# Three stacked layers on one core: the modulation's weighted sum moved from TensorE to VectorE, and the last experts' outputs added from 32-row strips

## The reference

```python
x = layer_ab(x, ...)      # norm, projection, two attentions (indexed top-k and sliding window), output projection
x = layer_cd(x, ...)      # norm, projection, compressed / selected / window attention, latent attention, output
mod = silu(c) @ w_ada + b_ada                 # c: 1024 numbers, w_ada: 1024 x 6144
sh1, sc1, g1, sh2, sc2, g2 = split(mod, 6)
h = rms_norm(x, norm1_g) * (1 + sc1) + sh1;   z = h @ w_in
x = x + g1 * (concat([diff_attention(z), multiscale_pool(z)]) @ w_out)
h = rms_norm(x, norm2_g) * (1 + sc2) + sh2
x = x + g2 * hierarchical_moe(h, ...)         # 32 experts of 1024 -> 512 -> 1024, two of them for each token
return rms_norm(x, final_g)
```

## Time and profile before

| | us |
|---|---|
| median of 3 runs | 978.06 (977.4 to 981.19) |
| profiled execution, its own time | 980.98 |
| span of the profiled execution | 978.9 |
| TensorE busy | 817.0 (83% of the span) |
| VectorE busy | 308.2 (31%) |
| ScalarE busy | 170.8 (17%) |

### The profile page before, as it was taken

How to read it: one execution, slowest core, us unless ns; L and a number is a source line. 1 busy time by engine, 2 the same in 40 slices (tenths; PEclk the granted TensorE clock), 3 DMA queues, 4 the chain that set the end, 5 groups by cost and what they waited for, 6 DMA issues and landing times.

```text
span 978.9 us, 13367 instructions
## 1 busy us (share of the span) xinstructions
PE 817.0 (83%) x5617; PEld 477.2 (49%) x5617; DVE 308.2 (31%) x786; ACT 170.8 (17%) x477; POOL 39.7 (4%) x36
## 2 busy tenths in 40 slices
PE   5999899999999899998887998686777767587665
PEld 3544554455567544455454755353444535354332
DVE  1476541127755423125443121211211111111112
ACT  3121540213255401004111010000000000000001
POOL 0110000011600000000000000000000000000000
PEclk9999998999999999999997999897998889998789
DMA  9963791243502475445465999999999999999994
GB/s 345 393 241 121 276 344 59 96 166 118 200 35 98 150 253 187 172 171 204 147 234 213 428 384 428 428 429 428 428 428 428 429 428 428 428 428 427 428 426 163
DMA packets 53387, 284.39 MB, mean 291 GB/s; under 512 B 2656, under 2 KB 7136, under 8 KB 40416
## 3 DMA queue, kind: packets, MB, share of 16 engines
q1 hardware_dynamic: 53344, 283.81, 73.2%
HBM read 282.75 MB, written 1.05 MB: 290 GB/s over the span
## 4 chain that ended last, share of the span: by engine, by line
PE 56%; DMA 33%; DVE 4%; ACT 2%; issue 2%; POOL 1%; SPq 1%; DVEq 0%; POOLq 0%
DMA ring<-in_up_w 30%; PE banks L1627 14%; PE banks L1748 14%; PE banks L2049 7%; PE banks L1707 4%; DMA ring<-in_down_w 3%; PE banks L1729 2%; PE banks L1654 2%; PE banks L1691 2%; PE banks L2095 2%; PE banks L1735 1%; POOL rs L512 1%; DMA ring<-in_ab_w 1%; PE banks L1606 1%; PE banks L2032 1%
## 5 line engine op out<-in xcount | busy, mean ns | idle before, releaser
L2049 PE MATMUL banks<-ring,QT 128*32 128x256 f32 x1952 | 148.1, 451 | 85.4 <-DMA ring<-in_up_w 84.6
L1748 PE MATMUL banks<-ring,hT 128*128 128x512 f32 (+4 forms) x384 | 157.3, 564 | 5.0 <-DMA ring<-in_ab_w 2.5
L2049 PEld LDWEIGHTS banks<-ring,QT 128*32 128x32 f32 x1952 | 78.1, 125 | 153.0 <-issue 95.1
L1627 PE MATMUL banks<-ring,hT 128*128 128x512 f32 x320 | 141.1, 600 | 7.5 <-ACT hT L536 5.1
L1748 PEld LDWEIGHTS banks<-ring,hT 128*128 128x128 f32 x384 | 72.2, 192 | 76.8 <-issue 68.8
L1627 PEld LDWEIGHTS banks<-ring,hT 128*128 128x128 f32 x320 | 60.9, 192 | 82.8 <-issue 76.7
L1518 DVE TENSOR_TENSOR QT<-banks,MOD 32x256 f32<-32x256 f32 x128 | 53.8, 420 | 140.3 <-PE banks L2095 139.0
L2095 PE MATMUL banks<-ring,QT 128*32 128x256 f32 x992 | 68.3, 420 | 15.6 <-ACT QT L828 12.4
L1509 DVE TENSOR_TENSOR QT<-QT,banks 64x256 f32<-64x256 f32 x32 | 13.5, 423 | 198.0 <-ACT QT L821 198.0
L512 POOL TENSOR_TENSOR rs<-st,mhalf 128x1 f32<-128x1 f32 (+7 forms) x27 | 32.5, 1204 | 933.7 <-DVE st L1561 467.1
L821 ACT ACTIVATE QT<-banks 64x256 f32<-64x256 f32 x32 | 12.0, 375 | 299.9 <-PE banks L2049 299.9
(11 more groups left out here) (344 smaller groups left out, 693.5 us busy)
## 6 DMA issues: line engine op xcount, KB each, us to landing
ring<-in_up_w SPq DMA_DIRECT2D x31, 2048.0 KB, 23.4
ring<-in_gate_w SPq DMA_DIRECT2D x30, 2048.0 KB, 18.9
ring<-in_down_w SPq DMA_DIRECT2D x30, 2048.0 KB, 21.8
ring<-in_ada_w SPq DMA_DIRECT2D x12, 2048.0 KB, 9.0
ring<-in_ab_w SPq DMA_DIRECT2D x4, 2048.0 KB, 20.2
ring<-in_cd_w SPq DMA_DIRECT2D x4, 2048.0 KB, 9.4
ring<-in_in_w SPq DMA_DIRECT2D x4, 2048.0 KB, 11.2
ring<-in_ab_out_w SPq DMA_DIRECT2D x2, 2048.0 KB, 10.5
```

The source lines that it names most:

```text
L1627: ins = pe.matmul(bank[j % 4][:, 0:n], hT[:, k, t * P:(t + 1) * P], w[:, k, :], start=(k == 0), stop=(k == KD - 1))
L1748: ins = pe.matmul(bank[b][:, 0:n], hT[:, k, t * P:(t + 1) * P], w[:, k, :], start=(k == 0), stop=(k == KD - 1))
L2049: return pe.matmul(bank[1][CAP * j:CAP * j + CAP, 0:256], XG[:, k, CAP * s:CAP * s + CAP], wk[:, :, 2 * (j % 2):2 * (j % 2) + 2], start=(k ...
```

## The change

Modulation: `ada_parts`, ScalarE's copy and `silu_c` go. VectorE makes the weighted sum of a chunk's eight slices by itself (`weigh`, eight linked operations of 128x512) into one of two halves of `extra`; TensorE's `ada_sum` adds the partitions with `share` = 1. Chunk 0 is weighed before part 0, chunks 1 to 6 beside `about` and `cdin`, 7 to 11 beside `cdout` and `win`, and the sums are placed between the groups of these projections. The load order changes with it.

Experts: for experts 30 and 31 the down product, whose four strips of 32 rows hold the four column quarters, is gated by one operation (`GATE_LAST`, `YE_LAST`) and added by eight 32-row, 256-column matmuls in two waves of four row strips (`add_last`), with the turned weights repeated on four strips (`on_strips`, `turn_last`). Experts 28 and 29 are added before expert 31's gate and up products, with 64 rows. At the end each tile's sum of squares is one operation of 1024.

```diff
-        add_ada(0, 7)
+        add_ada(0, 1)
         add_cols("about", ab_out_w, D)
+        add_ada(1, 7)
         for c in range(3):
             add_piece("cdin", cd_w, CD_AT, CD_WIDTHS, c)
...
-        add_ada(7, 10)
         add_cols("cdout", cd_out_w, D)
+        add_ada(7, 8)
         chunks.append(("rows", [(0, D, 1, norm_rows[:, 0:1]), (D, D, 1, norm_rows[:, 2:3])], ("final_row", 1)))
-        add_cols("win", in_w, 2048)
-        add_ada(10, 11)
+        add_ada(8, 10)
+        add_cols("win", in_w, 2048, (0, 2))
+        add_ada(10, 12)
+        add_cols("win", in_w, 2048, (2, 4))
...
-        add_ada(11, 12)
         add_cols("wout", out_w, D)
...
+            def weigh(c, ks=range(KD)):
+                if ks[0] == 0:
+                    arrived(v, f"ada{c}")
+                    if c > 1:
+                        v.wait_ge(*upto("ada_s", c - 1))
+                w = weights(f"ada{c}")[:, :].rearrange("p (k n) -> p k n", k=KD)
+                acc = ada_acc(c)
+                for k in ks:
+                    by = cs[:, 1, k:k + 1]
+                    if k == 0:
+                        ins = v.tensor_scalar(acc, w[:, k, :], by, None, ALU.mult)
+                    else:
+                        ins = v.scalar_tensor_tensor(out=acc, in0=w[:, k, :], scalar=by, in1=acc, op0=ALU.mult, op1=ALU.add)
+                    link(ins, "ada_mm" if k == KD - 1 else "dve")
...
-            attention(0, after=ada_rows)
-            for t in range(NT):
-                turned_rows("abm", t)
-            add_and_norm("about", "cd", "cdx", col="cd_col")
+            weigh(0)
...
+            attention(0, after=lambda u: ada(0) if u == 4 else None)
+            turned_rows("abm", 0)
+            weigh(1)
+            turned_rows("abm", 1)
+            def beside_first(n):
+                if n == 0:
+                    weigh(2)
+                elif n == 1:
+                    ada(1)
+                    weigh(3)
+                elif n == 2:
+                    ada(2)
+                elif n == 3:
+                    weigh(4, range(0, 4))
+                elif n == 4:
+                    ada(3)
+                elif n == 6:
+                    weigh(4, range(4, 8))
+            add_and_norm("about", "cd", "cdx", col="cd_col", beside=beside_first)
+            weigh(5)
+            ada(4)
+            weigh(6)
+            ada(5)
...
+            turned_rows("cdm", 0)
+            weigh(7)
+            turned_rows("cdm", 1)
...
+            def beside_second(n):
+                if n == 0:
+                    weigh(8)
+                elif n == 1:
+                    ada(7)
+                    weigh(9)
+                elif n == 2:
+                    ada(8)
+                elif n == 4:
+                    ada(9)
+            add_and_norm("cdout", "e1", "e1x", rows_=(1, 0), beside=beside_second)
             link(v.tensor_scalar(MOD[:, 0, :], weights("rows")[:, D:2 * D], math.sqrt(D), None, ALU.mult), "final_row")
+            weigh(10)
+            weigh(11)
...
-                if c is not None:
-                    ada_parts(c)
                 fill(u)
...
-            attention(0, ada_during)
+            attention(0, fill=lambda u: ada_sum(0) if u == 3 else None)
-            project("about", D, first_outputs)
+            project("about", D, first_outputs, ada_sums({1: 1, 2: 2, 3: 3}))
...
+            pe.wait_ge(*upto("about_x", 4))
+            ada_sum(4)
             project_cd(1, 0, 0)
+            ada_sum(5)
...
             project_cd(1, 1, 1)
+            ada_sum(6)
...
-            project("cdout", D, second_outputs)
-            project("win", 2048, normed_rows("e1", "e1x"))
+            project("cdout", D, second_outputs, ada_sums({1: 7, 2: 8, 3: 9}))
+            project("win", 2048, normed_rows("e1", "e1x", 9), ada_sums({1: 10, 3: 11}))
...
+                if e >= NE - 2:
+                    v.wait_ge(*upto("g_gl", 4))
+                    if e == NE - 1:
+                        v.wait_ge(*upto("g_wave", 8))
+                    v.tensor_tensor(YE_LAST, bank[2][:, 0:256], GATE_LAST, ALU.mult).then_inc(sem("g_ye"), 1)
+                    return
...
+            def add_last(i):
+                pe.wait_ge(*upto("g_swc", QUADS + 1 + i))
+                pe.wait_ge(*upto("g_ye", NE - 1 + i))
+                for wave in range(2):
+                    if i or wave:
+                        pe.wait_ge(*upto("g_wave", 8 * i + 4 * wave))
+                    for t in range(NT):
+                        for half in range(2):
+                            n = 2 * half + (t + wave) % 2
+                            strip = slice(CAP * n, CAP * n + CAP)
+                            pe.matmul(bank[4 + 2 * t + half][:, 256 * (n % 2):256 * (n % 2) + 256], SWT_LAST[i][strip, t, :],
+                                      YE_LAST[strip, :], start=False, stop=bool(i and wave))\
+                              .then_inc(sem("sums" if i and wave else "g_wave"), 1)
...
+                    if last_quad(q) and s in (1, 2):
+                        turn_last(s - 1)
                     turn_hidden(q, s)
                     if last_quad(q) and s == 2:
+                        add_outputs(q, 2)
                         gate_up(q, 3)
+                    if last_quad(q) and s == 3:
+                        add_last(0)
                     down(q, s)
```

More of the change, by code:

```diff
@@ L217, in build @@
         SEL, SW, SWT = spare(0), spare(256), spare(512)
+        SW_LAST = SEL
+        SWT_LAST = [GX[:, 256 * i:256 * i + 256].rearrange("p (t n) -> p t n", t=NT) for i in range(2)]
+        GATE_LAST, YE_LAST = GX[:, 512:768], GX[:, 768:1024]
         chunks = []
@@ L223, in rows, with add_cols @@
             return w.rearrange("(p k) n -> p k n", k=k)
-        def add_cols(tag, w, total, k=KD):
-            for c in range(-(-total // 512)):
+        def add_cols(tag, w, total, some=None, k=KD):
+            for c in range(*(some or (0, -(-total // 512)))):
                 n = min(512, total - 512 * c)
@@ L583, in evac_PT, with attention @@
                 act.activation(PTB[:, u % 2, 0:nb, :], banks[:, 4:4 + nb, :], ACT.Copy).then_inc(sem("ptA"), 1)
-            def attention(part, ada=lambda u: None, after=lambda u: None, early=lambda: None):
+            def attention(part, after=lambda u: None, early=lambda: None):
                 lo, hi = U0[part], U0[part + 1]
@@ L658, in _ @@
             take_ab(5, 1, ACT.Silu)
-            attention(0, ada_during)
+            attention(0)
             for t in range(NT):
@@ L844, in _ @@
                             take_tokens(e // 4 + 1, half)
[L845 to L847 removed]
+                for t in range(NT):
+                    act.wait_ge(*upto("sums", 2 * t + 2))
+                    sumsq(banks[:, 4 + 2 * t:6 + 2 * t, :], st[:, t:t + 1], "sum_ss",
+                          Y[:, t, D:2 * D].rearrange("p (c n) -> p c n", c=2))
             with act.Else():
@@ L925, in add_x, with add_and_norm @@
                     link(v.tensor_tensor(Y[:, t, cols], X[:, t, cols], MOD[:, scale, cols], ALU.mult))
-            def add_and_norm(tag, name, turned, gate=None, rows_=None, col=None):
+            def add_and_norm(tag, name, turned, gate=None, rows_=None, col=None, beside=lambda n: None):
                 scale = None if rows_ is None else rows_[0]
@@ L1223, in _ @@
                        "cmp_in")
+            ada(6)
             for t in range(NT):
@@ L1366, in _ @@
                 go(v.tensor_copy(QT[0:96, 2 * j:2 * j + 2, :], bank[4 + j % 4][0:96, :]), "dq_Tv")
-            attention(2, after=ada_rows)
-            for t in range(NT):
-                turned_rows("cdm", t)
+            attention(2)
+            turned_rows("cdm", 0)
+            weigh(7)
+            turned_rows("cdm", 1)
             a = SM["lambdas"][0]
@@ L1629, in project, with normed_rows @@
                         ins.then_inc(sem(tag + "_mm"), 1)
-            def normed_rows(name, tag):
+                        beside(j)
+            def normed_rows(name, tag, chunk=None):
                 def ready(t):
                     pe.wait_ge(*upto(name + "_xn", t + 1))
+                    if t == 1 and chunk is not None:
+                        pe.wait_ge(*upto("ada_v", chunk + 1))
                     turn_rows(tag, 0, t)
```

147 lines of the change are left out of this document (81 added, 66 removed).

## The result

The changed kernel takes **994.94 us** (median of 4 runs, 993.64 to 998.64) against 979.40 (977.40 to 981.19) for the kernel before beside it: ratio 1.0165, 95% interval 1.0128 to 1.0203. It is slower by some 16 us, where I forecast 978.3 and a range up to 985. The profiled execution spans 991.6 us instead of 978.9, at a mean granted clock of 0.916 instead of 0.935. These two differ by 12.7 us only, since the profiled execution of the kernel before was one of its slowest (980.98) and that of the changed kernel its fastest (993.64).

The account below looks back on a forecast made before the run. TensorE was taken to bound the first half, the full load queue the experts from 586 to 960 us. Terms -22.2 + 10.0 + 11.8 + 1.8 + 1.3 - 2.4 = +0.3 us gave 978.3 us, range 968 to 985.

Parts of the forecast that it names:

- The load order at `cdin`: First `cdin` chunk, issued behind a load waiting for `about`'s last group, holds TensorE up: +11.8 us, lower clock behind it +1.8.
- Modulation chunk 10 in `win`: Chunk lands 14.2 us after `cdout`'s end, its sum ready at 19.7 where TensorE comes at 18.5: +1.3 us (0 to 3).
- TensorE's clock: After the `cdin` wait the clock falls to its lower level: +1.8 us (0 to 3.5); no other place counted in the sum.
- the chain: Attention units: product, next transposes, their evacuation by ScalarE, next product, about 4.1 us a unit; -22.2 us over the attention parts.
- rival 3: TensorE falls to its lower clock within the thinner attention parts, costing 5 to 12 us: 986 us; chance 14%.
- My own sign of it: First attention part: a granted clock under 0.9 over it would show the forecast wrong.
- My argument against it: Third attention part before: TensorE 24.50 of 27.50 us busy, with gaps of 1.1 us, kept the full clock.
- Summing products: Eleven stand between groups of `about`, `cdin`, `cdout` and `win`, 0.91 us each with nothing to hide them: +10.0 us.
- VectorE's weighing at 0: Beside the projections and in VectorE's gaps: 5.4 us a chunk, 65 us in all, taken as 0, up to +3.
- Last experts: End of the kernel: one gating instead of four, strip sums in two waves, 1024-wide squares: -2.4 us (+0.7 to -3.5).
- Hidden, with about 1 us to spare: 64-row products and turned strips (3.4 + 0.9 us) before the last gate and up products cost nothing; +1 at low clock.
- The other terms: Attention units -22.2, summing products +10.0 and last experts -2.4 us: 14.6 us of gain together.

Follow-up runs that it names:

- run 1: Changed kernel with modulation chunks 1 to 3 loaded ahead of the two chunks of `about` instead of behind them: 981.96 us, ratio 1.0044 to the kernel before.
- run 2: Changed kernel with modulation chunk 7 loaded ahead of `cdout` and chunk 10 ahead of `win`'s first chunk: 988.94 us, ratio 1.0105 to the kernel before.
- run 3: Changed kernel with the load-order edits of run 1 and run 2 together: 974.11 us, ratio 0.9975 to the kernel before.
- run 7: Run 3's kernel with the 64-row products adding experts 28 and 29 moved ahead of expert 30's gate and up products: 966.98 us, ratio 0.9894 to the kernel before.
- run 11: The same kernel as run 3, timed again in another group of runs: 973.24 us, ratio 0.9967 to the kernel before.
- run 12: Run 10's kernel with the 12 summing products 32 columns wide instead of 512, output not the reference's: 956.80 us, ratio 0.9790 to the kernel before.
- run 13: Run 10's kernel with only the first and last of VectorE's eight weighing steps per chunk, output not the reference's: 963.84 us, ratio 0.9873 to the kernel before.
- run 8: Run 3's kernel with only the first and last of VectorE's eight weighing steps per chunk, output not the reference's: 971.32 us, ratio 0.9918 to the kernel before.
- run 4: Kernel before with only the change's part at the last two experts: 977.54 us, ratio 1.0004 to the kernel before.
- run 9: Run 4's kernel with the 64-row products moved ahead of expert 30's gate and up products: 974.83 us, ratio 0.9971 to the kernel before.
- run 6: Run 3's kernel with 16 unread filler products in TensorE's waits, 10 in the first attention part, 6 in the third: 966.41 us, ratio 0.9870 to the kernel before.
- run 10: Run 3's kernel with run 6's 16 filler products and run 7's moved 64-row products: 965.11 us, ratio 0.9868 to the kernel before.
- run 14: Run 10's kernel with four more filler products in the last two units of the fourth attention part: 962.75 us, ratio 0.9856 to the kernel before.

## Why the prediction was wrong

The sum was +0.3 us, the trace has +12.8. Two steps of it failed. The lower clock in and behind the thinned attention parts was put at 0 and measured as 6.2 us (7.5 with the compressed keys' products). The wait for modulation chunk 10 in `win`, with the clock behind it, was put at +1.3 and measured as +7.9. Together they came out 14.1 us above the forecast, all other terms together 1.6 below it.

- **The load order at `cdin`** (+11.8, clock +1.8): right in mechanism, place and size. Trace 12.4 and 2.0, run 1 11.8 in all. Without this step the forecast would have been 964.7 and further off.
- **Modulation chunk 10 in `win`** (+1.3, 0 to 3): the term of the sum that was most mis-sized. The trace has 4.9 us of wait and 3.0 of lower clock, and run 2 gives back 5.9. I took TensorE's arrival right (18.5 us after `cdout`'s end) and the chunk's wrong: I took 14.2 us for a landing, as of the second of a pair; the load took 16.7, in a queue whose share was 0.95 to 1.01 from 385 to 400 us, with three more loads issued before it had landed. Weighing then took 6.0 us instead of 5.4. And I gave this wait no clock of its own, though I had done so for the one at `cdin`.
- **TensorE's clock.** The attention units do what the chain said: 4.2 us a unit, the third part -5.6, the fourth -4.0, the last product of the first part within 0.5 us. What failed is the sum on top of it: it counts the lower clock at one place, behind the wait at `cdin`, and leaves the thinned parts to a rival of 14%. It came in every profile of the change that had no filler at the end of the first part, in five of seven at the end of the third, and lasted into the first projection group each time: +0.7, +2.5, +1.5, and 1.5 within the first part (from unit 7's product to `about`), 6.2 in all in the trace; with 1.3 at the compressed keys, where the change does nothing and which may be chance, 7.5. So rival 3, at 14%, came true besides the forecast. My own sign of it, a clock under 0.9 over the first part, was just missed (0.90 from 99 to 141 us), while the start of the full queue came 17.3 us later than before, instead of within the 4 us that I named. My argument against it, that the third part before had gaps of 1.1 us and kept the full clock, was read from one execution; runs 3, 7 and 11 show that the same code falls in one execution and not in the next.
- **Summing products** (+10.0): right; 9.5 in the trace, 8.3 in run 12 for fifteen sixteenths.
- **VectorE's weighing at 0**: right by run 13 to within about 3 us, though a chunk took 6.0 us; run 8 leaves it open whether it holds where the clock falls.
- **Last experts** (-2.4): the trace has -1.4 from expert 30's gate and up products to the end of the span (33.4 us instead of 34.8). The end behind expert 30's down product gained 2.8 us (1.6 in run 4), where 2.4 were worked out. "Hidden, with about 1 us to spare" failed: I read expert 31's stretched 7.59 us as a wait for weights that would take up all 4.1 us of added products, and it took 2.7; 1.4 lie on the path. Run 4 finds no gain, run 9 one of 2.8 us once the products stand in TensorE's wait of about 7 us for expert 30's weights. The trace of the changed kernel shows -4.6 after the start of the full queue: beside the 1.4, 1.3 lie between the first load of the full queue and the first into the ring (10.5 us instead of 11.8), and some 1.9 stay unexplained.

Of the 16 us, shown by experiment are the two orders, 18 us. That is more than the whole loss, so with these waits gone the change gains 0.25 to 0.33%. The other terms promised 14.6 us; most of what is missing is the clock, which the filler gives back to about 1%, its own cost taken off (run 6 against 3; run 10 against 11 is as much, the moved products with it). How the clock decides in a given execution isn't settled here; I don't have runs that tell which of the thinned stretches starts it, or why the kernel before is hit less often.

## What to carry to other kernels

When chunks move in a ring that is filled in order, write down for each chunk which one it waits for, and look at the one issued behind it: moving three modulation chunks ahead of two others was worth 12 us, and moving two more some 6. A wait on TensorE cost its length and, behind it, 2 to 3 us at the lower clock: price both, at every wait and not only at the longest. Taking work out of a part that has gaps can lower the clock, so the gain must be worked out at either level, and a gap that cannot be closed may be filled with idle products. One profile at full clock does not say that the next execution keeps it: look at the single times, and whether they fall into groups, before reading a median.

## What the runs showed of the hardware

- Products that nobody reads (16 of 128x512, 0.86 us each) made the kernel 1% faster. The single times of the three kernels with them and nothing left out (runs 6, 10 and 14) spread by 1.9 to 4.8 us over four to six executions each, those of the kernel with both orders alone by 5.7 (run 3) and 14.0 (run 11) over twelve.
- The granted clock fell to 0.50 behind idle times of 1.1 to 1.8 us between matmuls (1.83 us ahead of unit 6's product in the changed kernel's profile), stayed there while TensorE was busy 9.99 of 12 us (run 11), and the fall came at different units in different executions of the same instructions. Executions of one kernel (run 7) fell into two groups 11 us apart.
- Four 64-row products of 512 columns took 3.65 us (eight records), nearly the 3.70 of four 128-row ones (921.10 in the kernel before): half the rows saved nothing here. Eight 32-row products of 256 columns (16 records) in two waves of four strips took 1.56 us.
- A 2 MB load issued 0.6 us behind another took 16.7 us to land, where such pairs had taken 13.6 and 13.7, with more loads issued before it had landed.
- A multiply-add of VectorE over 128x512 took 0.78 us from start to start in a linked chain of seven (5.48 us), where I had estimated 0.7 from the 1.23 us of a 1024-wide one.
